# Residual chains of a two-block transformer kernel: first chunks pulled ahead of weight splits and small steps, and the last two squares and output products redistributed

## What is computed

```python
def rms_norm(x, g):
    return x * lax.rsqrt(jnp.mean(x * x, axis=-1, keepdims=True) + EPS) * g
def modulate(h, shift, scale):
    return h * (1.0 + scale) + shift
def swiglu(h, w_in, w_out):
    gate, up = jnp.split(h @ w_in, 2, axis=-1)
    return (jax.nn.silu(gate) * up) @ w_out
```

## Time and profile before

| what | value |
|---|---|
| median of three runs | 1625.07 us (1623.83 to 1627.56) |
| the profiled execution, its own time | 1625.11 us |
| its span in the trace | 1623.3 us (1.8 us less than its time) |
| PE (TensorE matmul) busy | 1603.9 us, 99% of the span |
| DVE (VectorE) busy | 833.5 us, 51% |
| ACT (ScalarE) busy | 493.5 us, 30% |
| POOL (GpSimd) busy | 135.3 us, 8% |
| granted TensorE clock, mean | 0.997 of full speed |

### The profile page before, as it was taken

One profiled execution on the slowest core, in us unless ns is written; L12 is line 12 of the kernel. 1 busy time (PEld: TensorE's weight loads), 2 busy tenths in 40 slices (PEclk: granted clock), 3 DMA queues, 4 the chain that ended last, 5 costly groups with the idle time before them and its releaser, 6 DMA issues.

```text
span 1623.3 us, 19912 instructions
## 1 busy us (share of the span) xinstructions
PE 1603.9 (99%) x8122; PEld 1362.0 (84%) x8122; DVE 833.5 (51%) x1007; ACT 493.5 (30%) x561; POOL 135.3 (8%) x114
## 2 busy tenths in 40 slices
PE   8999999999999999999999999999999999999998
PEld 6899999878888888888888888888988888888887
DVE  5897754674334344464544444346456544544352
ACT  4553264522212233332221222321323221222231
POOL 0100000030000000030000003135006000000000
PEclk9999999999999999999999999999999999999999
DMA  9544511212232223313222223332212222222331
GB/s 381 186 164 158 206 53 52 78 68 89 102 103 95 73 88 103 109 65 112 82 103 103 78 84 104 97 146 101 78 52 80 102 103 103 81 100 71 98 100 68
DMA packets 29320, 171.38 MB, mean 106 GB/s; under 512 B 3152, under 2 KB 3408, under 8 KB 15568
## 3 DMA queue, kind: packets, MB, share of 16 engines
q1 hardware_dynamic: 24912, 153.80, 27.3%
q0 software_dynamic: 4352, 16.78, 3.1%
HBM read 168.47 MB, written 2.10 MB: 105 GB/s over the span
## 4 chain that ended last, share of the span: by engine, by line
PE 73%; issue 22%; DMA 2%; DVE 1%; ACT 1%; SPq 0%; POOL 0%; POOLq 0%; DVEq 0%
PE bank L509 73%; DMA mod_w<-in_mod 2%; ACT w_hi L1160 0%; DVE mod_sum L1587 0%; SPq L342 0%; PE bank L809 0%; POOL root L404 0%; PE bank L753 0%; DVE a_lo L1996 0%; DVE w_lo L1948 0%; DVE tmp L2004 0%; PE bank L699 0%; PE bank L1042 0%; SPq L345 0%; DVE y_gla L1975 0%
## 5 line engine op out<-in xcount | busy, mean ns | idle before, releaser
L1566 DVE TENSOR_TENSOR w_lo<-w_raw,w_hi 128x2048 fp32r<-128x2048 f32 x142 | 327.7, 2308 | 386.7 <-ACT w_hi L1160 386.6
L509 PE MATMUL bank<-a_hi,w_hi 128*128 128x512 f32 x1248 | 488.4, 391 | 2.8 <-DVE a_lo L1996 1.9
L509 PE MATMUL bank<-a_hi,w_lo 128*128 128x512 f32 x1248 | 485.7, 389 | 0.0
L509 PE MATMUL bank<-a_lo,w_hi 128*128 128x512 f32 x1248 | 485.6, 389 | 0.0
L1160 ACT ACTIVATE w_hi<-w_raw 128x2048 fp32r<-128x2048 f32 x144 | 275.5, 1913 | 560.1 <-PE bank L509 559.4
L509 PEld LDWEIGHTS bank<-a_hi,w_hi 128*128 128x128 f32 x1248 | 234.3, 188 | 54.1 <-issue 3.3
L509 PEld LDWEIGHTS bank<-a_hi,w_lo 128*128 128x128 f32 x1248 | 234.2, 188 | 48.8
L509 PEld LDWEIGHTS bank<-a_lo,w_hi 128*128 128x128 f32 x1248 | 234.3, 188 | 48.5 <-issue 0.5
L509 PE MATMUL bank<-g_hi,w_lo 128*128 128x512 f32 x528 | 205.4, 389 | 0.0
L509 PE MATMUL bank<-g_hi,w_hi 128*128 128x512 f32 x528 | 205.4, 389 | 0.0
L509 PE MATMUL bank<-g_lo,w_hi 128*128 128x512 f32 x528 | 205.4, 389 | 0.0
(11 more groups left out here) (287 smaller groups left out, 1619.3 us busy)
## 6 DMA issues: line engine op xcount, KB each, us to landing
w_raw<-in_ffn_in SPq DMA_DIRECT2D x66, 1024.0 KB, 4.8
w_raw<-in_ffn_out SPq DMA_DIRECT2D x24, 768.0 KB, 4.2
mod_raw<-in_mod POOLq DMA_DIRECT2D x16, 1024.0 KB, 5.5
w_raw<-in_ffn_out SPq DMA_DIRECT2D x24, 640.0 KB, 4.0
w_raw<-in_gla_in SPq DMA_DIRECT2D x12, 1024.0 KB, 4.7
w_raw<-in_mix_in SPq DMA_DIRECT2D x10, 1024.0 KB, 4.8
mod_w<-in_mod SPq DMA_DIRECT2D x8, 1024.0 KB, 18.2
w_raw<-in_gla_out SPq DMA_DIRECT2D x4, 1024.0 KB, 4.8
```

The lines of the kernel that those rows point to most:

```text
L509: return pe.matmul(out, lhs, rhs, start=first, stop=last, skip_group_check=True)
L1566: V.tensor_tensor(flat(w_lo[s]), flat(w_raw[s]), flat(w_hi[s]).bitcast(F32), ALU.subtract).then_inc(lo_done[s], 1)
```

## The change

At the residual chains: PAIR_EARLY goes, and both chains use its order under the name PAIR_ORDER. In `residual_roots(1)` the wait for the spread root and `y_by_root(1, 0)` go ahead of the four small steps; VectorE adds xT of chunk 1 itself there, and GpSimd starts at chunk 2, after its second root. `x_lower(0)` goes ahead of `y_by_root(1, 1)`, and x_lower follows y_by_root at a distance of one chunk in place of two. TensorE's `keep_busy` after the sums is 12 in place of 18. In chain n = 0 the order becomes norm(0), half split, norm(1), lower_mod(0), lower_mod(1), y_by_root(3), and then norm(m), y_by_root(m + 2), lower_mod(m) for m = 2 to 7; norm(m) now waits for lower_mod(m - 1).

At the end: VectorE adds tmp[2], the square of chunk 6, to sq_sum between its sums of chunks 6 and 7, so TensorE sums tmp[3] alone after the last square. Chunk 3's product goes from GpSimd to VectorE, and the stores run 0, 1, 2, 3, 4, 5, 7, 6.

```diff
-OUT_REST = (3, 7)
-OUT_ORDER = (0, 1, 2, 4, 3, 5, 6, 7)
+OUT_REST = (7,)
+OUT_ORDER = (0, 1, 2, 3, 4, 5, 7, 6)
...
-PAIR_EARLY = ((0, 0), (1, 0), (0, 1), (1, 1), (0, 2), (0, 3), (1, 2), (0, 4), (1, 3), (0, 5), (0, 6), (0, 7),
-              (1, 4), (1, 5), (1, 6), (1, 7))
-PAIR_ORDER = ((0, 0), (0, 1), (1, 0), (0, 2), (1, 1), (0, 3), (0, 4), (1, 2), (0, 5), (1, 3), (0, 6), (0, 7),
+PAIR_ORDER = ((0, 0), (1, 0), (0, 1), (1, 1), (0, 2), (0, 3), (1, 2), (0, 4), (1, 3), (0, 5), (0, 6), (0, 7),
...
             inverse_root(PAIRS)
-            add_scaled(1, (1, 2))
             inverse_root(PAIRS, 2 * PAIRS)
-            add_scaled(1, range(3, KD))
+            add_scaled(1, range(2, KD))
...
-                for u, k in PAIR_ORDER if roots_at else PAIR_EARLY:
+                for u, k in PAIR_ORDER:
...
-                pe.wait_ge(sum_step, cnt.next(sum_step, KD - CPU))
+                pe.wait_ge(sum_step, cnt.next(sum_step, KD - 1))
                 token_sums(4, 0, sq_sum, T, True, False)
                 keep_busy(0, 3)
-                for c in range(CPU):
-                    pe.wait_ge(y_squared, 3 * KD + c + 1)
-                    m = token_sums(4, 0, tmp[2 + c], T, False, c == CPU - 1)
-                m.then_inc(sums_ready, 1)
+                pe.wait_ge(y_squared, 3 * KD + CPU)
+                token_sums(4, 0, tmp[3], T, False, True).then_inc(sums_ready, 1)
...
             term_sums(1)
-            keep_busy(0, 18)
+            keep_busy(0, 12)
...
                 dve.wait_ge(root_done, cnt.next(root_done))
+                if n:
+                    dve.wait_ge(roots_ready, cnt.next(roots_ready))
+                    y_by_root(1, 0)
                 dve.wait_ge(sums_ready, cnt.next(sums_ready))
...
-                dve.wait_ge(roots_ready, cnt.next(roots_ready))
+                if n == 0:
+                    dve.wait_ge(roots_ready, cnt.next(roots_ready))
...
-                if m == 0:
-                    dve.wait_ge(y_scaled, KD * n + 1)
-                    V.tensor_tensor(xT[:, 0], xT[:, 0], y[:, 0], ALU.add).then_inc(x_added, 1)
+                if m <= n:
+                    dve.wait_ge(y_scaled, KD * n + m + 1)
+                    V.tensor_tensor(xT[:, m], xT[:, m], y[:, m], ALU.add).then_inc(x_added, 1)
...
-            for m in range(KD):
+            def norm_mod(m):
+
                 dve.wait_ge(x_added, m + 1)
...
-                if m == 0:
-                    lo_half(1, 1)
-                    lower_mod(0)
-                if m + 3 < KD:
-                    y_by_root(0, m + 3)
-                if m >= 2:
-                    lower_mod(m - 1)
-            lower_mod(KD - 1)
+
+            norm_mod(0)
+            lo_half(1, 1)
+            norm_mod(1)
+            lower_mod(0)
+            lower_mod(1)
+            y_by_root(0, 3)
+            for m in range(2, KD):
+                norm_mod(m)
+                if m + 2 < KD:
+                    y_by_root(0, m + 2)
+                lower_mod(m)
...
+                    if first_square and c == 0:
+
+                        dve.wait_ge(y_squared, 3 * KD + 1)
+                        dve.wait_ge(sum_step, cnt.now(sum_step))
+                        V.tensor_tensor(sq_sum[:], sq_sum[:], tmp[2][:], ALU.add).then_inc(sum_step, 1)
...
-            for m in range(KD + 2):
+            x_lower(0, lambda m: col("ffn1_g", m))
+            y_by_root(1, 1)
+            for m in range(2, KD + 1):
                 if m < KD:
                     y_by_root(1, m)
-                if m >= 2:
-                    x_lower(m - 2, lambda m: col("ffn1_g", m))
+                x_lower(m - 1, lambda m: col("ffn1_g", m))
```

More of the change, by code:

```diff
@@ L2028, in x_roots, with sum_pair @@
                 dve.wait_ge(roots_copied, cnt.next(roots_copied))
-            def sum_pair(banks, chunks, half, to_x, j, squares):
+            def sum_pair(banks, chunks, half, to_x, j, squares, first_square=False):
                 dst = xT if to_x else y_ffn
@@ L2127, in out_body @@
                         chunks = [4 * i + 2 * j + c for c in range(CPU)]
-                        sum_pair((4 + 2 * j, 5 + 2 * j), chunks, True, to_x, j, last_ffn and not (final and j == 1))
+                        sum_pair((4 + 2 * j, 5 + 2 * j), chunks, True, to_x, j, last_ffn and not (final and j == 1),
+                                 last_ffn and final and j == 1)
                 def hidden(t, m0, c):
```

## The result

The changed kernel is slower: 1630.11 us in the median of 14 runs (1627.25 to 1632.65), against 1625.72 us in the median of 14 of the kernel before (1623.83 to 1627.56). The ratio is 1.0023, with a 95% interval of 1.0016 to 1.0031. The forecast was 1627.8 us, 2.7 us more; the ratio says 3.7 us more, and the medians say 4.4. The median lies 0.3 us above the range that was given.

The account below looks back on a forecast made before the run. With TensorE busy 99% of the span, only the two residual chains and the tail could change the time. Chain 0 +3.1, chain 1 +0.5 and the end -0.9 summed to +2.7 us: 1627.8 us, range 1622.3 to 1629.8.

Parts of the forecast that it names:

- Chain 0: First residual chain: turns of 3.35 us with lower_mod held by GpSimd's addition make block (1, 4) later, +3.1 us.
- the five blocks named: Chain 0: TensorE was to stand before blocks (0, 3) to (0, 7), some 4 us together.
- GpSimd first by 0.12 us: Chain 0: GpSimd's addition starts ahead of lower_mod at the shared ports and holds it; +3.1 us, against -0.8 otherwise.
- the ring: Chain 0 loop: norm(m) waits for lower_mod(m - 1), lower_mod(m) for ScalarE's a_hi of the same chunk; turn 3.35 us if held.
- Chain 1: Second residual chain: an earlier start, but the root of x spread behind the tenth block instead of the ninth; +0.5 us.
- the limit of 703.6: Chain 1: the first two blocks may start anywhere up to 703.6 without effect, as block (0, 1) starts at 706.3.
- The end: Tail behind the last matmul: eight fewer matmuls on tmp and no dip in the stores; -0.9 us, between -0.7 and -1.3.
- the -0.2 for the dip: Tail: the 0.2 us dip in the stores' rate, where chunk 3 waited for GpSimd, was to go.
- VectorE first at the ports: Rival: a lead of 0.12 us is not enough for GpSimd, VectorE keeps the ports; -1.8 us, 1623.3 us, chance 0.16.
- the one with the clock up at the end: Rival: VectorE keeps the ports and the clock stays up at the end, shortening the spread; -2.7, 1622.4 us, chance 0.14.
- The moves do nothing: Rival: x_lower(0) is held by GpSimd's root, stands only change place, only the end gains; 1624.2 us, chance 0.05.
- A fall of the clock into chain 0's stands: Rival: the granted clock goes to half while TensorE stands in chain 0, costing 1.6 us more; 1629.4 us, chance 0.2.

Follow-up runs that it names:

- turned: Changed kernel with y_by_root(m + 2) issued behind lower_mod(m) in chain 0 from chunk 2 on; 1626.75 us, ratio 1.0012 to the kernel before.
- apart: Changed kernel with norm(m) ahead of lower_mod(m - 1) from chunk 3 and y_by_root two chunks ahead in chain 0; 1625.87 us, ratio 0.9999 to the kernel before.
- c0_alone: Kernel before with only chain 0's new order from the change; 1630.09 us, ratio 1.0030.
- c1_alone: Kernel before with only chain 1's new order from the change and keep_busy of 12; 1626.09 us, ratio 1.0005.
- early: Kernel before with chain 0 reordered: norm(0), norm(1), lower_mod(0), then the half split, norms one chunk ahead of subtractions; 1624.11 us, ratio 0.9991.
- end_alone: Kernel before with only the new end from the change; 1625.14 us, ratio 0.9995.
- swap: Changed kernel with blocks (1, 3) and (0, 5) swapped in PAIR_ORDER, so the root is spread one block earlier; 1627.72 us, ratio 1.0013 to the kernel before.

## Why the prediction was right, and where it was not

**Chain 0** came out as worked: the turn of 3.35 us was 3.37, the stands stood ahead of the five blocks named, (0, 7) was to start at 352.2 and started at 352.22. The open point, GpSimd first by 0.12 us, fell to the side that was taken. No row showed that lead and the other side had 0.30, so this was a choice between two bounds, and in part luck. That a shared pair of ports goes to the one that starts first ("SBUF — State Buffer", "SBUF: two separate sides", in the Trainium skill) agrees now down to 0.12 us: lower_mod 1.73 us in the held turns of the change, 0.75 in `turned`, where no addition runs beside it. The rule does not come out for GpSimd's root on 128x4, and there the measurement decides: in chain 1 the root started first, by 0.04 us (704.77 against 704.81), and lasted 1.01 us, and x_lower(0) took 0.75 us. The loss needs both parts: the hold without the ring costs next to nothing (`apart`: a lower_mod of 1.78 us, one stand of 0.23), and the ring without the hold, with y_by_root in it, 0.75 us (`turned`).

**Chain 1**: +0.5 was worked out, +0.56 measured. That x_lower(1) would be held was worked out, and was so (1.72 us, GpSimd first by 0.12). That the start itself is worth nothing is borne out by the two profiles with the clock up and down (starts of 5.87 and 6.54 us after M1; the limit of 703.6 is 6.9).

**The end**: -0.9 was -0.79 at equal clock. The -0.7 for the matmuls on tmp was 0.74; the -0.2 for the dip was 0.05, since at full clock there was no dip to lose. The profile of before had half clock in its spread, and I used its rows without asking what the tail is at full clock; so the profiled pair shows -1.53, of which 0.74 is luck.

**The sum** was 1 us short, +2.7 against +3.7 by the ratio. The terms of the span at equal clock are 3.2 + 0.6 - 0.8 = 3.0. Two things are not in it. First, I took what lies outside the span as fixed, 1.8 us. It is 2.17 us in the mean of the changed kernel's runs and 1.80 in those of before; 1.8 in c0_alone, c1_alone and early, 2.01 in end_alone, 2.16 to 2.18 in those that hold all parts. That is 0.36 us from a term that I had not costed. Why is open; no run was made for it. Second, the clock. Runs of before with a mean granted clock of 0.999 took 1624.15 us, and those at 0.995 1627.1 (11 and 19 runs); of the change 1627.5 and 1630.7 (4 and 4). So at these two clocks they differ by 3.3 and 3.6 us, which the 3.0 and the 0.36 account for. At 0.996 to 0.998 the change has only five runs, and they lie 4.2 to 5.1 us over those of before; so a fall of the clock may cost the change more. Why the means differ by 3.8 and the medians by 4.4 stays open: no trace of such a run of the change was taken.

**The rivals.** VectorE first at the ports: out, by the trace. Of the one with the clock up at the end only the clock came true: the spread was at full clock in the profiled run. The moves do nothing: out, x_lower(0) was not held by the root, and the time rose. A fall of the clock into chain 0's stands as a cost of the change: not shown, and not ruled out for the runs without a trace. The mean clock of the changed kernel's runs (0.9969) is that of before (0.9965), and where a profile had half clock in chain 0 it began in the small sums and the keep-busy matmuls, ahead of the stands; in the four profiles with the ring (after, c0_alone, turned, swap) it was full from 335 to 356 us. So in the profiles the loss comes by the sum, not by this rival.

## What to carry to other kernels

In a pipeline over two engines with two buffers, keep the producer one chunk ahead in program order; here that alone gave back 3.75 us (`apart`). Pulling a consumer up to its producer makes a ring that pays every engine's time, and every hold, on every turn, even where it makes an early chunk come sooner. And before two engines are given work in the same stretch, work out which of them starts first at shared ports: a lead of 0.12 us went with a hold of 1 us per chunk here, and it was the order of two independent instructions that set it. A start that is made earlier is worth only what the next dependent block and the next fixed point (here the spread root) let through. And before a tail's rows are used as terms, look at its clock: both the length of the spread and the dip in the stores were the clock's.

## What was not expected of the hardware

The time between the span and the whole moved by 0.36 us between programs that differ in a few instructions (0.2 of it with the new end alone). And the clock is a larger source of scatter than any part of this change but one: among the runs of the kernel before, those at 0.995 took 2.9 us more than those at 0.999, so a single profile is one draw, and its stretches at half clock have to be marked before its rows are used as terms. In `turned` it stood at half for these two microseconds in chain 0 (the seventh value), where the kernel before had 1.00:

```profile
326.00:327.00 1.00, 1.00 (x6) 1.00 (x6) 0.57 (x4) 0.00 (x0) 0.25 (x1) 0.50 0.00 0
327.00:328.00 1.00, 1.00 (x7) 1.00 (x7) 0.23 (x1) 0.00 (x0) 0.76 (x1) 0.50 0.00 0
```
